# In the experts ScalarE makes a block's gate activation before the high part of the same slot

## The chip, the cores and the metric

One core of a Trainium2 chip runs the whole program. The metric is the device time of one execution in microseconds (us). The engines are named TensorE (PE in the profile, PEld for its weight loads), VectorE (DVE), ScalarE (ACT), GpSimd (POOL) and SyncE (SP), which issues most DMAs.

## What is computed

A trunk of two layers over 256 tokens of width 2048, all in float32. Each layer has an attention mixer and then a feed-forward part. In layer 0 that part is one dense SwiGLU; in layer 1 it is a mixture of 8 experts, of which every token takes its best two:

```python
def swiglu(x, wg, wu, wd):
    return (jax.nn.silu(x @ wg) * (x @ wu)) @ wd

def moe(xn, w_router, wg, wu, wd):
    ...
    for e in range(N_EXPERTS):
        y = y + comb[:, e:e + 1].astype(t.dtype) * swiglu(t, wg[e], wu[e], wd[e])
```

An expert has gate and up matrices of 2048 x 1408 and a down matrix of 1408 x 2048. The change touches the experts alone.

## The kernel before

**Pieces.** All weights come as pieces of 128 x 1024 float32 (512 KB), 920 of them, of which the last 528 are the experts' (8 times 66). SyncE loads each into one of 11 buffers of a ring (`load`, L394 to L400), as soon as TensorE has used the piece that was there 11 pieces before (semaphore `used`). ScalarE copies the piece to a rounded "high part" (`high`, L1032 to L1035: it waits for the landing, then one activation, tile `w_high`). VectorE makes the "low part", the piece less its high part (`low`, L1374 to L1378, tile `w_low`), which waits for the high part. TensorE then multiplies three times for each row block: high by high, high by low, low by high (`three`, L598 to L600), and counts the piece as used.

**Slots.** The order on each engine is written out by hand. An expert is a loop over 66 slots, 0 to 65; seven experts run in a hardware loop (`more` true), the last is written out once with 58 slots (`more` false). In slot i TensorE works on the expert's piece i + 8 (those from 66 on are the next expert's first eight), and ScalarE and VectorE prepare piece i + 14 (`ahead(e, i + 8, more)`, which adds `LEAD` = 6). So a piece prepared in slot i is multiplied in slot i + 6.

**Blocks.** The gate and up products come in 6 blocks: blocks 0 to 4 take 8 pieces each and give 256 columns of gate and 256 of up, block 5 takes 4 pieces and gives 128 and 128. Block 1 ends in TensorE's slot 7, block 2 in 15, 3 in 23, 4 in 31, 5 in 35, and the next expert's block 0 in slot 65 (`E_BLOCK_END = {7: 1, 15: 2, 23: 3, 31: 4, 35: 5, 65: 6}`). The down products follow in slots 36 to 57, eleven row blocks for each of 4 column blocks, two row blocks to a piece.

**From a block to the down products.** Five steps on three engines, each at a place fixed by its slot:

1. ScalarE, in the slot in which the block ends: `silu` (L1307 to L1310) waits on `used` for the block's last piece, then makes the gate activation (tile `silu_gate`).
2. VectorE, first thing in the next slot: `gated` (L1742) multiplies it with the up half (tile `h_blocks`).
3. TensorE, after the products of slot 3, 11, 19, 27, 34 or 37 for blocks 0 to 5 (`E_TURN`): transposes of `h_blocks` (L974), which wait for step 2.
4. ScalarE, one slot after the transposes and behind that slot's high part: the transposed block's high part (L1340, tile `hT_high`).
5. VectorE, two slots after the transposes and behind that slot's low part: its low part (L1771, tile `hT_low`). TensorE waits for this one before the down piece that first needs the block: for block 5 that is piece 5 of the down matrix, in slot 41.

So for block 5: block end and activation in slot 35, `gated` in 36, transposes after 37, `hT_high` in 38, `hT_low` in 39, needed in 41.

Each engine works its instructions in the order of the program, and an instruction that waits for a semaphore holds all behind it. The second pass over the experts (L1360 to L1362) runs only if one expert gets more than 128 tokens; here it does not run.

Of the kernel before, what the change touches and what calls it, by code (L numbers as in the profile page):

```python
# [101 lines left out]
def gu_width(b):  # L102
    return GW if b < 5 else P


def gu_chunks(b):
    return (2 * b, min(2 * b + 2, FC))


def gu_end(b):  # L110

    return 8 * (b + 1) if b < 5 else GU_PIECES
# [7 lines left out]
def dn_end(d):  # L120

    return GU_PIECES + (FC * (d + 1) - 1) // 2 + 1
# [29 lines left out]
def expert_groups(more, n_pass):  # L152


    tp, high = {}, {}
    for i in range(SLICE_PIECES):
        for kind, at in (("t", E_TURN), ("gather", E_GATHER if more else {}), ("st", expert_selt(more, n_pass))):
            if i in at:
                tp[kind, at[i]] = len(tp)
                if kind != "st":  # L160
                    high[kind, at[i]] = len(high)
    return tp, high


def trunk(nc, x, x_t, positions, gains, w_in, q_norm_dil, k_norm_dil, w_out, norm_ffn, ffn_dense, w_router, ffn_moe,
# [38 lines left out]
    with ExitStack() as ctx:  # L204
# [819 lines left out]
        def _(act):  # L1024
# [7 lines left out]
            def high(piece, shift=0):  # L1032

                act.wait_ge(raw_full[piece % RING], shift * (16 * SLICE_PIECES // RING) + 16 * (piece // RING + 1))
                act.activation(WH[:, piece % RING, :], RAWS[:, piece % RING, :], ACT.Copy).then_inc(high_done, 1)  # L1035
# [263 lines left out]
            def moe_pass(n_pass):  # L1299
                s = PASS[n_pass]  # L1300

                def ahead(e, i, more):

                    if more or i + LEAD < SLICE_PIECES:
                        high(s["piece"] + i + LEAD, e)

                def silu(e, b):  # L1307
                    act.wait_ge(used, e * SLICE_PIECES + (s["piece"] + gu_end(b % GU_BLOCKS) + SLICE_PIECES * (b // GU_BLOCKS)))
                    w = gu_width(b % GU_BLOCKS)
                    act.activation(SG[:, b % 2, 0:w], G[b % 2][:, 0:w], ACT.Silu).then_inc(silu_done, 1)  # L1310

                def gathered_high(count, k, q):
                    act.wait_ge(tp_ready, count + 1)
                    act.activation(XTH[:, 4 * q:4 * q + 4, 0:SLOTS], TP[k % 2][:, :].rearrange("p (c n) -> p c n", c=4),
                                   ACT.Copy).then_inc(tp_high, 1)

                def expert(e, more):
                    tp, _ = expert_groups(more, n_pass)
                    TP_MORE = s["tp_more"]
                    for i in range(SLICE_PIECES if more else NEXT_GU):  # L1320
                        ahead(e, i + 8, more)
                        if i in E_BLOCK_END:
                            silu(e, E_BLOCK_END[i])
                        if i in E_DOWN_END:
                            d = E_DOWN_END[i]
                            act.wait_ge(used, e * SLICE_PIECES + (s["piece"] + dn_end(d)))
                            if n_pass == 0:

                                if d == 0:
                                    act.wait_ge(cur_done, e + 1)  # L1330
                                act.activation(Y[:, d * NB:(d + 1) * NB], DN[d % 2][:, :], ACT.Copy,  # L1331
                                               scale=GC[:, 0:1]).then_inc(dn_free, 1)
                            else:
                                act.activation(YH[d % 2], DN[d % 2][:, :].rearrange("p (c n) -> p c n", n=P), ACT.Copy).then_inc(y_high, 1)
                        if i - 1 in E_TURN:
                            b = E_TURN[i - 1]
                            n = s["tp"] + tp["t", b]
                            c0, c1 = gu_chunks(b)
                            act.wait_ge(tp_ready, e * TP_MORE + (n + 1))
                            act.activation(HTH[:, c0:c1, 0:SLOTS], TP[n % 2][:, 0:(c1 - c0) * P].rearrange("p (c n) -> p c n", n=P),  # L1340
                                           ACT.Copy).then_inc(tp_high, 1)
                        if i - 1 in E_GATHER and more:
                            q = E_GATHER[i - 1]
                            n = s["tp"] + tp["gather", q]
                            gathered_high(e * TP_MORE + n, n, q)

                if n_pass:
                    for i in range(LEAD):
                        high(s["piece"] + i)
                for q in range(KD // 4):  # L1350
                    gathered_high(s["tp0"] + q, s["tp0"] + q, q)
                for j in range(8):
                    ahead(0, j, True)
                silu(0, 0)
                with act.Fori(0, N_EXP - 1) as e:
                    expert(e, True)
                expert(N_EXP - 1, False)

            moe_pass(0)
# [519 lines left out]
```

## Time and profile before

| | |
|---|---|
| median of three runs | 1936.08 us (1935.62 to 1936.53) |
| the profiled execution's own time | 1933.81 us |
| its span in the profile | 1931.7 us |
| TensorE (PE) busy | 1911.5 us, 99% |
| VectorE (DVE) busy | 1348.4 us, 70% |
| ScalarE (ACT) busy | 1163.4 us, 60% |
| chain that ended last | PE 92%, DVE 3%, DMA 2%, ACT 2% |

The share of busy time is a mean over stages. The experts take the last 750 us of the span, from about 1185 us on. Experts are numbered 0 to 7 here, and expert 3 starts its slot 0 near 1468 us. In a row of the timeline the time in square brackets is how long the engine sat idle before the instruction, and what ended that; a row without brackets followed the one before without idle time. Rows that merge several instructions say x2 or x3.

### The profile page before, as it was taken

Reading aid. Unit: us, or ns where it says so; the run is one execution under the profiler, and the core shown is the slowest. Engines: PE = TensorE matmul, PEld = TensorE weight load, DVE = VectorE, ACT = ScalarE, POOL = GpSimd, SP = SyncE. Lnnn points to the kernel's source line nnn. Section 1 sums busy time; section 2 is a strip of 40 time slices with the busy share of each in tenths; the row PEclk is TensorE's granted clock in tenths of the full one; section 3 lists DMA queues with packets and bytes.
Section 4 is the critical chain, followed back from the end, with each engine's and each line's share of the span. In section 5 each row is a group of like instructions: output and inputs, shape, how many; then the busy total and the mean of one; then the engine's idle time right before and its main releaser. Section 6 shows DMA issues by size and latency. Waiting matters only on the chain.

```text
span 1931.7 us, 27170 instructions
## 1 busy us (share of the span) xinstructions
PE 1911.5 (99%) x9176; PEld 1597.2 (83%) x9176; DVE 1348.4 (70%) x1580; ACT 1163.4 (60%) x1496; POOL 135.6 (7%) x152
## 2 busy tenths in 40 slices
PE   9999999999999999999999999999999999999998
PEld 7788888888888888888887888888888888888887
DVE  7776654554444555454657777898989898898996
ACT  7556543443433443444545557878878778787885
POOL 7300000000000000000200000000001000000101
PEclk9999999999999999999999999999999999999999
DMA  9555666666666666666665567999999999999997
GB/s 354 175 163 149 178 190 188 189 193 189 186 195 187 190 186 193 195 186 185 188 186 154 155 225 284 388 389 383 395 380 397 387 393 388 394 385 395 375 397 260
DMA packets 141588, 510.31 MB, mean 264 GB/s; under 512 B 15936, under 2 KB 15952, under 8 KB 140080
## 3 DMA queue, kind: packets, MB, share of 16 engines
q1 hardware_dynamic: 134288, 486.64, 72.3%
q0 software_dynamic: 7200, 22.39, 4.6%
q8 instruction: 56, 0.92, 0.2%
q14 instruction: 44, 0.36, 0.1%
HBM read 495.33 MB, written 13.64 MB: 263 GB/s over the span
## 4 chain that ended last, share of the span: by engine, by line
PE 92%; DVE 3%; DMA 2%; ACT 2%; issue 1%; SPq 0%; POOLq 0%; DVEq 0%; ACTq 0%
PE main L598 29%; PE main L600 29%; PE main L599 29%; DVE w_low L1377 1%; DMA raw_pieces<-in_w_in 1%; DMA raw_pieces<-in_ffn_moe 1%; PE transpose L934 1%; ACT w_high L1035 1%; PE transpose L616 1%; PE transpose L797 0%; PE transpose L974 0%; DVE heads_scratch L1417 0%; PE transpose L917 0%; DVE small L1418 0%; PE transpose L638 0%
## 5 line engine op out<-in xcount | busy, mean ns | idle before, releaser
L1377 DVE TENSOR_TENSOR w_low<-raw_pieces,w_high 128x1024 fp32r<-128x1024 f32 x919 | 1095.1, 1222 | 427.6 <-ACT w_high L1035 420.9
L1035 ACT ACTIVATE w_high<-raw_pieces 128x1024 fp32r<-128x1024 f32 x919 | 949.8, 1058 | 262.3 <-DMA raw_pieces<-in_ffn_dense 126.6
L598 PE MATMUL main<-w_high,xT_high 128*128 128x512 f32 (+1 forms) x1920 | 731.5, 381 | 2.5 <-DVE w_low L1498 0.9
L600 PE MATMUL main<-w_high,xT_low 128*128 128x512 f32 (+1 forms) x1920 | 721.5, 376 | 0.0
L599 PE MATMUL main<-w_low,xT_high 128*128 128x512 f32 (+1 forms) x1920 | 720.7, 375 | 0.0
L598 PEld LDWEIGHTS main<-w_high,xT_high 128*128 128x128 f32 x1920 | 361.8, 188 | 66.5 <-issue 3.3
L600 PEld LDWEIGHTS main<-w_high,xT_low 128*128 128x128 f32 x1920 | 361.6, 188 | 66.3
L599 PEld LDWEIGHTS main<-w_low,xT_high 128*128 128x128 f32 x1920 | 362.1, 189 | 62.8
L598 PE MATMUL main<-w_high,hT_high 128*128 128x512 f32 x832 | 329.9, 396 | 1.3 <-DVE hT_low L1771 1.2
L600 PE MATMUL main<-w_high,hT_low 128*128 128x512 f32 x832 | 324.6, 390 | 0.0
L599 PE MATMUL main<-w_low,hT_high 128*128 128x512 f32 x832 | 324.2, 390 | 0.0
L598 PEld LDWEIGHTS main<-w_high,hT_high 128*128 128x128 f32 x832 | 156.3, 188 | 35.0 <-DVE w_low L1377 3.9
L600 PEld LDWEIGHTS main<-w_high,hT_low 128*128 128x128 f32 x832 | 156.1, 188 | 33.3
L599 PEld LDWEIGHTS main<-w_low,hT_high 128*128 128x128 f32 x832 | 156.5, 188 | 30.4
L1259 ACT ACTIVATE silu_gate<-main,small 128x256 f32<-128x256 f32 (+1 forms) x48 | 19.3, 453 | 197.3 <-PE main L600 197.3
L588 POOL DMA_INDIRECT out_x<-attention_weights,result_rows x32 | 51.7, 1614 | 470.2 <-ACT attention_weights L1331 426.6
L1564 DVE TENSOR_TENSOR x_resid<-main,x_resid 128x512 f32<-128x512 f32 x32 | 20.6, 686 | 68.4 <-PE main L600 68.4
L554 POOL DMA_DIRECT2D heads_scratch<-in_q_norm_dil x1 | 0.6, 556 | 881.0 <-PE main L600 881.0
L1265 ACT ACTIVATE hT_high<-transpose 128x512 fp32r<-128x512 f32 (+1 forms) x24 | 13.5, 563 | 69.2 <-PE transpose L797 69.2
L1331 ACT ACTIVATE attention_weights<-main,slot_gates 128x512 f32<-128x512 f32 x32 | 22.0, 686 | 29.7 <-PE main L600 29.5
L1052 ACT ACTIVATE squares<-x_resid 128x512 f32<-128x512 f32 x32 | 20.2, 633 | 23.9 <-DVE x_resid L1564 18.2
L1063 ACT ACTIVATE xT_high<-transpose,gains_by_row 128x256 fp32r<-128x256 f32 x48 | 18.8, 475 | 21.7 <-PE transpose L616 21.7
(231 smaller groups left out, 812.7 us busy)
## 6 DMA issues: line engine op xcount, KB each, us to landing
raw_pieces<-in_ffn_moe SPq DMA_DIRECT2D x528, 512.0 KB, 6.4
raw_pieces<-in_ffn_dense SPq DMA_DIRECT2D x264, 512.0 KB, 3.7
raw_pieces<-in_w_in SPq DMA_DIRECT2D x96, 512.0 KB, 3.7
raw_pieces<-in_w_out SPq DMA_DIRECT2D x32, 512.0 KB, 3.6
x_resid<-in_x SPq DMA_DIRECT2D x4, 512.0 KB, 15.0
out_x<-x_resid POOLq DMA_DIRECT2D x4, 512.0 KB, 3.7
xn_rows<-token_major POOLq DMA_DIRECT2D x2, 1024.0 KB, 5.5
token_major<-in_x_t SPq DMA_DIRECT2D x1, 1024.0 KB, 10.0
```

The source lines that it names most:

```text
L588: pool.indirect_dma_start(out[d][:, :], bass.IndirectOffsetOnAxis(ap=RC[:, 0:1], axis=0), Y[:, cols], None, compute_op=ALU.add).then_inc(y ...
L598: pe.matmul(out_ap, lh[ls], rh[rs], start=first, stop=False)
L599: pe.matmul(out_ap, lh[ls], rl[rs], start=False, stop=False)
L600: return pe.matmul(out_ap, ll[ls], rh[rs], start=False, stop=last)
L616: ins = pe.transpose(TP[n % 2][:, (TILES * c + t) * P:(TILES * c + t + 1) * P], X[:, t, (2 * g + c) * P:(2 * g + c + 1) * P], IDN[:, :])
L934: ins = pe.transpose(TP[k % 2][:, i * P:(i + 1) * P], XG[:, c * P:(c + 1) * P], IDN[:, :])
L1035: act.activation(WH[:, piece % RING, :], RAWS[:, piece % RING, :], ACT.Copy).then_inc(high_done, 1)
L1052: act.activation(JUNK[:, :], X[:, t, d * NB:(d + 1) * NB], ACT.Square, accum_out=SSP[:, DBLOCKS * t + d:DBLOCKS * t + d + 1]).then_inc(sq_ ...
L1259: act.activation(SG[:, TILES * (b % 2) + t, 0:gu_width(b)], PAIR[b % 2][t][:, 0:gu_width(b)], ACT.Silu, scale=RSTD[1][:, t:t + 1]).then_in ...
L1331: act.activation(Y[:, d * NB:(d + 1) * NB], DN[d % 2][:, :], ACT.Copy, scale=GC[:, 0:1]).then_inc(dn_free, 1)
L1377: dve.tensor_tensor(WL[:, piece % RING, :], RAWS[:, piece % RING, :], WH[:, piece % RING, :], ALU.subtract).then_inc(low_done, 1)
L1564: dve.tensor_tensor(xs, PAIR[d % 2][t][:, :], xs, ALU.add).then_inc(dn_free, 1)
```

## The change

In ScalarE's slot loop of an expert, the call that makes the block's gate activation moves ahead of the call that makes the slot's high part. Nothing is added or removed. It touches the slots of `E_BLOCK_END`: six in each of seven experts, five in the last, 47 activations in all (the 48th, of the first expert's block 0, stands ahead of the loop).

```diff
                     for i in range(SLICE_PIECES if more else NEXT_GU):
-                        ahead(e, i + 8, more)
+
                         if i in E_BLOCK_END:
                             silu(e, E_BLOCK_END[i])
+                        ahead(e, i + 8, more)
                         if i in E_DOWN_END:
                             d = E_DOWN_END[i]
```

## Rows read from the trace of the kernel before

**Rows 1.** The page: TensorE's busy time, and the granted clock in 40 slices.
```profile
PE 1911.5 (99%) x9176; PEld 1597.2 (83%) x9176; DVE 1348.4 (70%) x1580; ACT 1163.4 (60%) x1496; POOL 135.6 (7%) x152
PEclk9999999999999999999999999999999999999999
```
**Rows 2.** Waits from 1200 to 1900 us: total us, times, longest.
```profile
ACT w_high L1035 <- DMA raw_pieces<-in_ffn_moe: 106.8, 302, 3.6
DVE w_low L1377 <- ACT w_high L1035: 67.3, 66, 3.4
...
ACT silu_gate L1310 <- PE main L600: 4.1, 8, 0.8
PEld main L598 <- DVE w_low L1377: 3.9, 7, 0.9
```
**Rows 3.** Waits from 1900 to 1903 us, in the last expert.
```profile
PEld main L598 <- DVE hT_low L1771: 0.2, 1, 0.2
```
**Rows 4.** Timeline of ScalarE, expert 3, slot 35: start us, us, instruction.
```profile
1517.04 1.06 ACT L1035 ACTIVATE w_high<-raw_pieces 128x1024 fp32r<-128x1024 f32 x1 [0.22 <-DMA raw_pieces<-in_ffn_moe]
1518.01 0.26 ACT L1310 ACTIVATE silu_gate<-main 128x128 f32<-128x128 f32 x1
```
**Rows 5.** Timeline of VectorE, expert 3, slots 33 to 39.
```profile
1515.67 3.69 DVE L1377 TENSOR_TENSOR w_low<-raw_pieces,w_high 128x1024 fp32r<-128x1024 f32 x3
1519.28 0.28 DVE L1742 TENSOR_TENSOR h_blocks<-main,silu_gate 128x128 f32<-128x128 f32 x1
1519.52 1.23 DVE L1377 TENSOR_TENSOR w_low<-raw_pieces,w_high 128x1024 fp32r<-128x1024 f32 x1
1520.66 0.42 DVE L1771 TENSOR_TENSOR hT_low<-transpose,hT_high 128x256 fp32r<-128x256 f32 x1
1520.99 3.49 DVE L1377 TENSOR_TENSOR w_low<-raw_pieces,w_high 128x1024 fp32r<-128x1024 f32 x3
1524.41 0.28 DVE L1771 TENSOR_TENSOR hT_low<-transpose,hT_high 128x128 fp32r<-128x128 f32 x1
```
**Rows 6.** Timeline of TensorE's matmuls, expert 3: the last of block 5.
```profile
1517.46 0.28 PE L600 MATMUL main<-w_high,xT_low 128*128 128x256 f32 x1
```
**Rows 7.** Timeline of TensorE's weight loads, expert 3, slots 40 and 41.
```profile
1524.10 0.19 PEld L600 LDWEIGHTS main<-w_high,hT_low 128*128 128x128 f32 x1
1524.81 0.19 PEld L598 LDWEIGHTS main<-w_high,hT_high 128*128 128x128 f32 x1 [0.53 <-DVE w_low L1377]
```
**Rows 8.** Timeline of ScalarE, expert 4, slot 35.
```profile
1612.08 0.28 ACT L1310 ACTIVATE silu_gate<-main 128x128 f32<-128x128 f32 x1 [0.23 <-PE main L600]
1612.25 0.38 ACT L1340 ACTIVATE hT_high<-transpose 128x256 fp32r<-128x256 f32 x1
```
**Rows 9.** Timeline of TensorE's matmuls, expert 4: the last of block 5.
```profile
1611.76 0.28 PE L600 MATMUL main<-w_high,xT_low 128*128 128x256 f32 x1
```
**Rows 10.** Timeline of ScalarE, expert 4, slots 15 and 16.
```profile
1582.03 1.06 ACT L1035 ACTIVATE w_high<-raw_pieces 128x1024 fp32r<-128x1024 f32 x1 [0.22 <-DMA raw_pieces<-in_ffn_moe]
1583.85 0.39 ACT L1310 ACTIVATE silu_gate<-main 128x256 f32<-128x256 f32 x1 [0.76 <-PE main L600]
1584.13 1.06 ACT L1035 ACTIVATE w_high<-raw_pieces 128x1024 fp32r<-128x1024 f32 x1
```
**Rows 11.** Timeline of VectorE, expert 4: the low part of slot 15.
```profile
1583.80 1.22 DVE L1377 TENSOR_TENSOR w_low<-raw_pieces,w_high 128x1024 fp32r<-128x1024 f32 x1
```
**Rows 12.** Timeline of TensorE's weight loads, expert 4: block 2's transposes, then slot 21's first.
```profile
1588.86 0.37 PEld L974 LDWEIGHTS transpose<-identity,h_blocks 128*128 128x128 f32 x2
...
1590.47 0.19 PEld L598 LDWEIGHTS main<-w_high,xT_high 128*128 128x128 f32 x1
```
**Rows 13.** Timeline of TensorE's matmuls in the two mixers: two long idle times.
```profile
64.17 1.08 PE L638 MATMUL transpose<-identity,token_major 128*128 128x128 f32 x4 [2.81 <-DVE token_major L1427]
...
1057.08 0.70 PE L660 MATMUL spread<-heads_scratch,incl 128*128 128x256 f32 x2 [1.28 <-DVE heads_scratch L1459]
```
**Rows 14.** Busy time in stretches: us, engines, granted clock (PEclk), DMA.
```profile
63.50:67.00 3.50, 2.83 (x9) 2.47 (x10) 1.78 (x2) 1.65 (x3) 2.77 (x9) 0.51 0.25 103
1050.00:1060.00 10.00, 8.72 (x41) 7.01 (x40) 8.56 (x14) 5.41 (x9) 0.00 (x0) 1.00 0.55 162
```

## The prediction, made before the changed kernel ran

> **What bounds the kernel.** I read the page first: TensorE is busy 99% of the span at the full clock in nearly every slice [rows 1], so an edit on ScalarE costs or gives only what it does to TensorE's few idle moments. The second view is the list of waits over the experts [rows 2]. ScalarE waits 302 times for a landing (106.8 us) and VectorE 66 times for a high part (67.3 us), and neither matters by itself, because both prepare a piece six slots before it is used. TensorE itself waits only in one kind of row: seven times, 3.9 us in all, longest 0.9, ended by VectorE; the last expert has an eighth of 0.2 [rows 3]. So there is one stop per expert. The third view, the timeline around one of them, says where: in expert 3 the weight load at 1524.81 comes 0.53 us late [rows 7], just after VectorE has ended block 5's `hT_low` at 1524.41 + 0.28 = 1524.69 [rows 5]. The profile names VectorE's next instruction as the one that ended the wait, but 1524.81 is 0.12 after the end of `hT_low`, which slot 41 needs. The weights of slot 41 were ready since 1519.36 (end of the third low part of the row at 1515.67).
>
> **What leads to that stop.** I follow VectorE back from 1524.41 [rows 5]. Low parts of slots 37 to 39, block 4's `hT_low`, the low part of slot 36, `gated` of block 5 and, before these, the low part of slot 35 follow each other with no idle time. The low part of slot 35 had to wait for its high part, which ScalarE ran from 1517.04 to 1518.10 after it had waited 0.22 us for the landing [rows 4]. From the start of that high part (1517.04) to the end of block 5's `hT_low` (1524.69) it is 7.65 us, of which the high part is 1.06 and the rest is VectorE at full load. Whatever delays the high part of slot 35 delays TensorE in slot 41, one for one.
>
> **What the change does there.** Slot 35 is a block end, so in the new order the high part stands behind an activation that waits for TensorE to end slot 35.
> - When does TensorE end it? In expert 3 the last matmul of block 5 starts at 1517.46 [rows 6]. Expert 4 shows what follows: last matmul at 1611.76 [rows 9], and the activation, which did wait there, at 1612.08 [rows 8], 0.32 later. So in expert 3 it can start at 1517.78, and ScalarE, free since 0.22 before 1517.04, now stands still for about 1 us although its piece has landed.
> - When does the high part follow? Behind the small activation the next instruction starts 0.17 later in expert 4 [rows 8]; behind the wide one of slot 15 a high part starts 0.28 later (1583.85 to 1584.13) [rows 10]. No row has a high part straight behind the small one. I take 0.22, nearest to both, with 0.15 and 0.32 as ends (0.32 is four hundredths more than the wide one needs).
> - The high part then starts at 1518.00 in place of 1517.04, 0.96 late. VectorE's chain has no idle time to give back, so `hT_low` ends at 1518.00 + 7.65 = 1525.65 and the load of slot 41 starts 0.12 later, at 1525.77. The load before it ends at 1524.10 + 0.19 = 1524.29 [rows 7]. The idle time becomes 1.48 us where it was 0.53.
>
> **The same in all eight.** Until now the stop hung on when the piece of slot 35 happened to land, which differs between experts: 0.2 to 0.9 us. In the new order the chain starts at TensorE's own last matmul of block 5 and ends at TensorE's slot 41, and what lies between is fixed: 0.32 + 0.22 + 7.65 + 0.12 = 8.31 us of chain, against 1524.29 - 1517.46 = 6.83 us of TensorE's own work. So each expert stops for 1.48 us. Where the high part used to run far ahead of TensorE, as in expert 4, it is delayed by more than in expert 3, but the old stop was shorter, and the new order ends at the same 1.48. The sum: 8 x 1.48 = 11.8 us new, less 3.9 + 0.2 = 4.1 us old, is +7.7 us. With the ends 0.15 and 0.32 for the step behind the activation the stop is 1.41 or 1.58, and the sum 7.2 or 8.5.
>
> **The step that the sum rests on** is that the high part can't pass the waiting activation. Rows 10 show one such hold: ScalarE stood idle for 0.76 us ahead of the activation of slot 15, and only then came the next high part. The Trainium skill says it outright (TensorE: Matmul & The Clock Gate, section "Architectural detail: the array is 16× 32×32, not 1× 128×128"): ScalarE's and VectorE's queues are strictly first in, first out, while TensorE may pull weight loads ahead. If a ready activation could pass a waiting one, the sum would be nothing in place of 7.7; the trace agrees with the page.
>
> **The other block ends** cost nothing that reaches TensorE. In slots 7, 15, 23, 31 and 65 either TensorE has ended the block before ScalarE comes to it (only 8 of the activations waited at all, 4.1 us together [rows 2]); then the activation fills part of a wait for a landing and the high part comes 0.3 us late at most. Or ScalarE is early and now waits longer. The worst I found is slot 15 of expert 4: the activation starts at 1583.85 as before, since TensorE sets it, and the high part, which ran at 1582.03, comes behind it at 1584.13, 2.10 late [rows 10]. Its low part can start at 1584.13 + 1.06 + 0.03 = 1585.22 in place of 1583.80 [rows 11], and end at 1586.44. TensorE takes up slot 21 at 1590.47 [rows 12]. That is 4.0 us of cover left. `gated` of block 2 moves by the same 1.42 us, to about 1586.8, and its transposes come at 1588.86 [rows 12]. Both costs are set at nothing; were the cover gone, such a slot would cost up to 2.1 us. Earlier gate activations bring nothing in these blocks, since their transposes have the same kind of cover. Block 5's own transposes get `gated` 0.96 us later, about when they are due, but a stop there only comes ahead of the stop in slot 41 and is part of it. No DMA is moved; SyncE's loads hang on TensorE's `used` alone, so they shift with TensorE and land no later relative to it.
>
> **Rivals.**
> 1. *No change.* The delayed high part of slot 35 is swallowed, since weights are ready six slots ahead and VectorE catches up. For it speaks the slack of the weights themselves (5 us in expert 3). Against it: VectorE's row has no idle time from slot 35 to 39, and what is late is not the weight but `hT_low` behind it. Time 1936.1. Chance 0.08. It becomes true if VectorE's chain has more than 0.9 us of idle time in the experts that stop now.
> 2. *Faster.* The activation in the gap of a landing wait saves ScalarE some 0.3 us a block, and the chain to slot 41 shortens until the old stops are gone: 4.1 us less, 1932.0. It needs TensorE to end block 5 before ScalarE arrives, and in expert 3 the last matmul starts 0.4 us after the high part does. Chance 0.02.
> 3. *Other block ends reach TensorE too.* If the delayed high parts of slots 7 and 15 eat the cover in the half of the experts where ScalarE is early, 4 more stops of up to 2.1 us come on top: 1943.8 + 8.4 = 1952.2. It decides only once 4.0 us of cover are gone. Chance 0.03.
> 4. *The clock falls.* After an idle time of 2.81 us in the first mixer [rows 13] the granted clock was 0.51, that is the lower level of 1.2 GHz, for the next 3.5 us [rows 14]; after 1.28 us in the second mixer [rows 13] it stayed at 1.00 [rows 14]. A stop of 1.48 us lies near the second. At the lower level half of 3.5 us is lost; eight times that is 14 us, 1957.8. Chance 0.02.
>
> **How the numbers follow.** The forecast is 1936.08 + 7.7 = 1943.8 us (for the profiled execution 1933.8 + 7.7 = 1941.5), with chance 0.85. The range for 8 times in 10 takes the ends 7.2 and 8.5, and adds for what one expert's rows can't tell of the others (another idle moment in VectorE's chain worth 0.35 us in each expert on the low side, 7.2 - 2.8 = 4.4; one slot's worn-out cover of 2.1 us on the high side, 10.6): 1940.5 to 1946.7. It leaves out all four rivals. A measurement of this kernel can tell about 0.2%, 3.9 us, from no change. Slower by more than that: the forecast and rivals 3 and 4, 0.90. Within: rival 1, 0.08. Faster: rival 2, 0.02.
>
> **What would show it.** In the waits of the new profile TensorE should have eight stops, all alike, near 1.5 us, at slot 41 (or split between block 5's transposes and slot 41); ScalarE's waits of `silu_gate` for TensorE should rise from 8 to well over 20; the expert's length should grow by 0.6 to 1.3 us each, with all growth between slots 35 and 41. If the stops stay unequal at 0.2 to 0.9, the chain as I read it is wrong; if they are equal but of another size, the step behind the activation is.

## The result and the profile after

| | before | after |
|---|---|---|
| median, 8 runs each | 1935.72 us | 1941.18 us |
| range | 1931.77 to 1937.0 | 1937.45 to 1943.17 |
| the profiled execution's own time | 1933.81 us | 1943.07 us |
| its span | 1931.7 us | 1941.0 us |

The medians lie 5.5 us apart. The ratio of the runs is 1.0031, with a 95% interval of 1.0023 to 1.0040, which makes the cost of the change 6.0 us, between 4.5 and 7.7. The ratios of this document leave out two executions that took far longer than all others (4983.57 us of the kernel in which only VectorE's order changes, 3789.71 us of the kernel before). The forecast was +7.7, slower; the range of 1940.5 to 1946.7 holds the time.

The two profiled executions lie 9.3 us apart, more than the medians. Of that, 2.2 us had come up before the experts: the first transposes of expert 0 start at 1191.02 after and at 1188.85 before. 1.6 us of it come up around the stop in the first mixer that [rows 13] show. The stop itself ended only 0.3 us later (64.49 against 64.17); 1.3 us more were lost behind it, where the granted clock stayed low for longer after the change. The third number from the end of a row is the granted clock, first before, then after:

```profile
67.00:70.50 3.50, 3.50 (x17) 2.91 (x17) 1.23 (x1) 1.05 (x4) 3.22 (x5) 1.00 0.57 135
```
```profile
67.00:70.50 3.50, 3.50 (x10) 2.68 (x9) 1.23 (x1) 0.46 (x1) 3.17 (x5) 0.57 0.52 146
```

The other 0.6 us are a longer wait of TensorE near 584 us (1.18 against 0.63). The program is the same in both kernels up to there, and among the traces of the other kernels of this document the experts' first transposes start anywhere from 1186.93 to 1191.11. So in what follows the experts are compared by a length of their own, from the first transposes of expert 0 to the last weight-high matmul of the down products. Before it runs from 1188.85 to 1923.79, 734.94 us. After, from these two rows of TensorE's timeline, it is 741.96 us, so the experts cost 7.0 us more:

```profile
1191.02 0.38 PE L974 MATMUL transpose<-identity,h_blocks 128*128 128x128 f32 x2
...
1932.98 0.39 PE L598 MATMUL main<-w_high,hT_high 128*128 128x512 f32 x1
```

The waits of the kernel after, from 1184 us on (us in total, times, longest); [rows 2, 3] hold the lines of before, for a window that starts at 1200:

```profile
ACT w_high L1035 <- DMA raw_pieces<-in_ffn_moe: 100.3, 258, 3.5
DVE w_low L1378 <- ACT w_high L1035: 79.2, 83, 2.4
...
ACT silu_gate L1310 <- PE main L600: 26.0, 24, 2.1
PEld main L598 <- DVE w_low L1378: 7.0, 7, 1.1
...
PEld transpose L974 <- issue: 3.8, 7, 0.7
PEld main L598 <- DVE hT_low L1772: 1.0, 1, 1.0
PEld transpose L974 <- DVE h_blocks L1743: 0.5, 1, 0.5
```

ScalarE's gate activation waits for TensorE 24 times in place of 9 (26.0 us, not 4.5, when the trace of before is taken from 1184 us on too). TensorE's weight loads wait in two places in each expert now: eight times 1.0 us in slot 41 (7.0 + 1.0) and eight times about 0.54 us at block 5's transposes (3.8 + 0.5). Before there was one place, with 4.1 us.

Expert 3, slot 35, on ScalarE after the change, against [rows 4]:

```profile
1519.97 1.06 ACT L1035 ACTIVATE w_high<-raw_pieces 128x1024 fp32r<-128x1024 f32 x1 [0.21 <-DMA raw_pieces<-in_ffn_moe]
1522.41 0.28 ACT L1310 ACTIVATE silu_gate<-main 128x128 f32<-128x128 f32 x1 [1.39 <-PE main L600]
1522.59 1.05 ACT L1035 ACTIVATE w_high<-raw_pieces 128x1024 fp32r<-128x1024 f32 x1
```

The same stretch on VectorE, against [rows 5]:

```profile
1523.67 1.22 DVE L1378 TENSOR_TENSOR w_low<-raw_pieces,w_high 128x1024 fp32r<-128x1024 f32 x1 [0.90 <-ACT w_high L1035]
1524.82 0.28 DVE L1743 TENSOR_TENSOR h_blocks<-main,silu_gate 128x128 f32<-128x128 f32 x1
1525.02 1.21 DVE L1378 TENSOR_TENSOR w_low<-raw_pieces,w_high 128x1024 fp32r<-128x1024 f32 x1
1526.15 0.41 DVE L1772 TENSOR_TENSOR hT_low<-transpose,hT_high 128x256 fp32r<-128x256 f32 x1
1526.48 3.48 DVE L1378 TENSOR_TENSOR w_low<-raw_pieces,w_high 128x1024 fp32r<-128x1024 f32 x3
1529.89 0.28 DVE L1772 TENSOR_TENSOR hT_low<-transpose,hT_high 128x128 fp32r<-128x128 f32 x1
```

And TensorE: the last matmul of block 5 (as [rows 6]), then the weight loads with the two stops (as [rows 7]):

```profile
1522.09 0.28 PE L600 MATMUL main<-w_high,xT_low 128*128 128x256 f32 x1
```
```profile
1525.22 0.14 PEld L974 LDWEIGHTS transpose<-identity,h_blocks 128*128 128x128 f32 x1 [0.52 <-issue]
...
1529.11 0.19 PEld L600 LDWEIGHTS main<-w_high,hT_low 128*128 128x128 f32 x1
1530.29 0.19 PEld L598 LDWEIGHTS main<-w_high,hT_high 128*128 128x128 f32 x1 [0.99 <-DVE w_low L1378]
1530.40 0.19 PEld L599 LDWEIGHTS main<-w_low,hT_high 128*128 128x128 f32 x1
```

Read in order: block 5's last matmul at 1522.09, the activation 0.32 later, the high part of slot 35 another 0.18 later, VectorE idle 0.90 for it and then at work without idle time up to 1530.17, and TensorE's load at 1530.29. The gated product ends at 1525.10 and the transposes' load follows at 1525.22, the first stop.

### The profile page after: what moved, and what is told of

Read it like the earlier page. It is cut to its first block, busy times and chain, and to the rows that moved or that the text cites. A ratio compares the mean times of both kernels' runs of the same rounds, so it can differ in the third digit from the quotient of the medians.

```text
span 1941.0 us, 27170 instructions
## 1 busy us (share of the span) xinstructions
PE 1915.0 (99%) x9176; PEld 1598.3 (82%) x9176; DVE 1347.8 (69%) x1580; ACT 1156.7 (60%) x1496; POOL 136.8 (7%) x152
## 4 chain that ended last, share of the span: by engine, by line
PE 91%; DVE 3%; POOL 2%; ACT 2%; issue 2%; DMA 0%; POOLq 0%; DVEq 0%
PE main L598 29%; PE main L600 29%; PE main L599 28%; DVE w_low L1378 1%; PE transpose L934 1%; ACT w_high L1035 1%; PE transpose L616 1%; PE transpose L797 0%; PE transpose L974 0%; PE transpose L917 0%; PE transpose L638 0%; DVE heads_scratch L1418 0%; DVE small L1419 0%; DVE hT_low L1772 0%; PE spread L660 0%
## 5 line engine op out<-in xcount | busy, mean ns | idle before, releaser
L1310 ACT ACTIVATE silu_gate<-main 128x256 f32<-128x256 f32 (+1 forms) x48 | 17.2, 358 | 26.1 <-PE main L600 26.0
```

## The experiments

The theory under test: all of the loss comes from slot 35, where the high part stands behind an activation that waits for TensorE, and VectorE's full queue carries the delay to block 5's low part in slot 41. The first rival: the other block ends share in it. The second: standing still costs on ScalarE as such, wherever VectorE stands. The third: the old stops are no fixed amount.

### Slot 35 alone, and all the others alone

```diff
-                        ahead(e, i + 8, more)
-                        if i in E_BLOCK_END:
+                        if i in E_BLOCK_END and i == 35:
+                            silu(e, E_BLOCK_END[i])
+                        ahead(e, i + 8, more)
+                        if i in E_BLOCK_END and not (i == 35):
                             silu(e, E_BLOCK_END[i])
```

> Only slot 35 has the new order; the five other block ends keep the old one. Theory (all of the loss comes from the high part of slot 35 standing behind the activation of block 5): the experts grow by the same 7.0 us as with the whole change (in its trace 9.2 us up to the last piece, of which 2.2 us lie ahead of the experts), each expert stops TensorE by 1.2 us between slots 35 and 41, in two parts, block 5's transposes and slot 41. ScalarE waits for TensorE ahead of the activation in slot 35 in all eight experts. Rival (the other block ends share in the loss): less than 5 us.

Measured over 10 runs: ratio 1.0026 (1.0016 to 1.0035) against the kernel before, +5.0 us. In its trace the experts take 741.71 us, 6.8 more than before, and TensorE's waits are those of the whole change (the timed runs alone, with 3.1 to 6.8 us, leave room for less than the rival's 5; the trace does not):

```profile
ACT silu_gate L1310 <- PE main L600: 13.1, 16, 1.9
PEld main L598 <- DVE w_low L1379: 7.0, 7, 1.0
...
PEld transpose L974 <- issue: 3.7, 7, 0.5
...
PEld main L598 <- DVE hT_low L1773: 1.0, 1, 1.0
PEld transpose L974 <- DVE h_blocks L1744: 0.5, 1, 0.5
```

So slot 35 makes the whole loss. The complement has the condition `i != 35` in both places.

> The complement: new order in slots 7, 15, 23, 31 and 65, old order in slot 35. Theory: the experts' time is that of the kernel before within 0.3 us, with stops of 0.2 to 0.9 us in slot 41 as before, although ScalarE waits for TensorE longer at these block ends and high parts come up to 2 us late there. Rival (these delays reach TensorE or reach slot 35 through VectorE's backlog): 2 us or more slower. Rival (the earlier activations help): over 1 us faster.

Measured over 10 runs: ratio 0.9996 (0.9987 to 1.0006), no change. But its trace has 2.3 us more in the experts (737.27 us), as much as the first rival asks for, all in slot 41 and at block 5's transposes of single experts. The expectation of 0.3 us failed, so two things were open: whether the old stops are the same in every execution, and whether the other ends set VectorE back.

### The kernel before, twice more

> The kernel before again, for a second trace of it. Open: its stops in slot 41 hang on when the piece of slot 35 lands. In its first trace they add up to 3.1 us over the eight experts, while the timed runs put the whole change at +5.5 us where its trace shows +7.0 in the experts. Theory (landings fall differently from execution to execution, and the first trace had few stops): other sizes of the eight stops, by up to 1 us in single experts, in the mean a sum of 4 to 5 us. Rival (the stops are the same in every execution): 3.1 us again, each within 0.1 us.

> The kernel before a third time. Theory: again other sizes of the eight stops, between 2 and 6 us in sum. Rival: 3.1 us as in the first trace.

The experts took 734.47 and 736.78 us, against 734.94 in the first trace. The waits of weight loads, first in the one, then in the other:

```profile
PEld main L598 <- DVE w_low L1377: 3.3, 7, 0.9
...
PEld main L598 <- DVE hT_low L1771: 0.2, 1, 0.2
```
```profile
PEld main L598 <- DVE w_low L1377: 5.1, 7, 1.1
...
PEld transpose L974 <- issue: 0.8, 1, 0.8
...
PEld main L598 <- DVE hT_low L1771: 0.2, 1, 0.2
```

Expert 1, for one, stopped for 0.90 us in the first trace and in these two for:

```profile
1336.06 0.19 PEld L598 LDWEIGHTS main<-w_high,hT_high 128*128 128x128 f32 x1 [0.32 <-DVE w_low L1377]
```
```profile
1337.80 0.19 PEld L598 LDWEIGHTS main<-w_high,hT_high 128*128 128x128 f32 x1 [1.06 <-DVE w_low L1377]
```

So the old stops add up to 4.1, 3.5 and 6.1 us of waits in the three traces. The texts above and below give 3.1 us for the first trace, and 2.6 to 4.9 us for all three: that counts TensorE's lost time, about 0.12 us less for each stop than the idle time of its loads (why is said in the part on the prediction). The expected mean of 4 to 5 us was too high (it is 3.5, and the experts' lengths have a mean of 735.4), but the sizes do vary, and not the new ones: in the new order the experts took 741.96 and 741.71. Against the mean of three the change costs 6.6 us in the experts, nearer to the 5.5 to 6.0 of the timed runs.

The old stops have a floor, too, which the prediction did not see. Where slot 35's piece lands early, the stop is 0.31 to 0.32 us all the same (seven cases in the three traces; 0.24 to 0.25 in the last expert, in each of them). Expert 4 of the first trace is one, and shows what sets it. ScalarE, first row, makes the high part of slot 36 behind block 5's activation, which waits for TensorE [rows 8]; VectorE, second row, stands idle for it ahead of slot 36's low part:

```profile
1612.52 1.06 ACT L1035 ACTIVATE w_high<-raw_pieces 128x1024 fp32r<-128x1024 f32 x1
```
```profile
1613.61 1.23 DVE L1377 TENSOR_TENSOR w_low<-raw_pieces,w_high 128x1024 fp32r<-128x1024 f32 x1 [0.30 <-ACT w_high L1035]
```

That low part starts 1.85 us after block 5's last matmul (1611.76), and 1.85 or 1.86 us after it in all ten cases of the floor. So the kernel before already has the fault that the change makes bigger: a high part behind an activation that waits. Before it is slot 36's high part, after it is slot 35's too.

### Slot 31 alone

As above with the condition `i == 31`.

> Only slot 31 has the new order. In the run with all ends but slot 35 in the new order, VectorE took up the low part of slot 35 without idle time before it in four experts (2, 3, 6, 7), never sooner than 2.13 us after block 4's transposes, though its high part was there up to 0.8 us sooner. Theory (ScalarE's wait in slot 31 sets VectorE back, and the backlog lasts to slot 35): with slot 31 alone the low part of slot 35 again starts no sooner than 2.13 us after block 4's transposes in any expert, and those experts stop by 0.3 to 0.4 us. Rival (the backlog comes from the earlier ends, slots 15 and 23): single experts start it at 1.6 to 1.9 us as in the kernel before.

In experts 1, 2, 3, 5 and 6 the low part of slot 35 started without idle time before it, each time 2.13 us after block 4's transposes; in the other three its own high part came later than that. Expert 6, VectorE in slots 32 to 36, where four low parts follow each other:

```profile
1799.63 4.62 DVE L1379 TENSOR_TENSOR w_low<-raw_pieces,w_high 128x1024 fp32r<-128x1024 f32 x4
1804.17 0.28 DVE L1744 TENSOR_TENSOR h_blocks<-main,silu_gate 128x128 f32<-128x128 f32 x1
```

The theory held: ScalarE's wait in slot 31 sets VectorE back, and the backlog lasts for the four slots to 35. It makes a floor under the stops, of 0.38 to 0.43 us in those experts (the loads' idle time), hardly above the 0.31 that the old order has anyway, and in sum nothing that shows: 735.27 us, in a single execution. In the whole change it is hidden, since slot 35's own wait sets VectorE's start at 3.11 us after block 4's transposes. What is left of the 2.3 us above is landings that fell late in that execution (experts 0, 1 and 4 began slot 35's high part behind a landing at 2.16, 1.93 and 1.80 us after block 4's transposes); the traces of before reach 2.25.

### The suspected cause doubled

```diff
+                        if i == 34:
+                            silu(e, E_BLOCK_END[35])
                         ahead(e, i + 8, more)
-                        if i in E_BLOCK_END:
+                        if i in E_BLOCK_END and i != 35:
                             silu(e, E_BLOCK_END[i])
```

> The suspected cause doubled: block 5's activation goes ahead of the high part of slot 34, one slot earlier still, so two high parts stand behind its wait; all other ends as before. Theory (each weight part that stands behind the wait sets VectorE's chain back by one low part, 1.14 us): TensorE is late by 1.23 + 1.14 = 2.4 us in each expert, most of it at block 5's transposes (1.5 us), 19 us in all, 14 to 16 us above the kernel before, about 1950. Rival (ScalarE has 0.2 us a piece to make up the delay, so the second part costs little): 1.4 us per expert, 7 to 8 us above. Rival (stops this long bring the lower clock): over 25 us above, with a granted clock below 1 in the experts.

Measured over 4 runs: 1948.95 us against 1936.59 beside it, ratio 1.0061 (1.0041 to 1.0081); the expected 14 to 16 us lie at the upper end of that interval, and in the trace the experts take 750.79 us, 15.9 more than before. The stops are now mostly at the transposes:

```profile
PEld transpose L974 <- issue: 11.6, 7, 1.7
...
PEld main L598 <- DVE w_low L1379: 6.9, 7, 1.0
...
PEld transpose L974 <- DVE h_blocks L1744: 1.6, 1, 1.6
PEld main L598 <- DVE hT_low L1773: 1.0, 1, 1.0
```

The step from one to two delayed high parts is 750.79 - 741.96 = 8.8 us, 1.10 per expert: one low part of VectorE (1.14 between starts), and not the 0.2 that ScalarE's share would be. How long ScalarE stood still did not matter: it was 2.91 us in slot 34 of expert 3 and 1.44 us in expert 0, and both met the same two stops (1.66 and 0.99 us). What stands behind its wait did. The clock did not fall, with loads idle for 1.66 us at a time (TensorE, 1200 to 1300 us: 98.19 busy, granted clock 1.00):

```profile
1200.00:1300.00 100.00, 98.19 (x472) 81.55 (x471) 86.66 (x93) 77.64 (x89) 7.50 (x5) 1.00 1.01 382
```

### VectorE's order, with the old and with the new order on ScalarE

In VectorE's slot 39 block 5's low part goes ahead of that slot's weight low part; `turned_block_low` holds the old lines word for word.

```diff
                         if b < GU_BLOCKS:
                             gated(b)
+                        if i == 39:
+                            turned_block_low(i)
                         ahead(e, i + 8, more)
...
-                        if i - 2 in E_TURN:
+                        if i - 2 in E_TURN and i != 39:
+                            turned_block_low(i)
```

> The old order on ScalarE; on VectorE, in slot 39 alone, the low part of block 5 (what TensorE waits for in slot 41) goes ahead of that slot's weight low part. Theory (the stop is VectorE's chain of weight low parts ahead of block 5's low part): that part comes 1.14 us earlier, the old stops of 0.1 to 0.8 us vanish, the experts take 3.1 us less, some 1932.6 us where the kernel before has 1935.7. Rival (the stop waits for the arrival of data, in ScalarE or the DMA, and VectorE's order is not what decides): stops as before, no change.

Measured over 9 runs: 1932.10 us, ratio 0.9985 (0.9975 to 0.9994); experts 732.40 us, 2.5 less than in the first trace where 3.1 were expected. No stop in slot 41 is left, but three at block 5's transposes, 1.0 us in all, in experts where slot 35's piece landed late; VectorE's row in expert 3 shows two weight low parts ahead of block 5's in place of three:

```profile
1521.68 2.35 DVE L1377 TENSOR_TENSOR w_low<-raw_pieces,w_high 128x1024 fp32r<-128x1024 f32 x2
1523.95 0.28 DVE L1750 TENSOR_TENSOR hT_low<-transpose,hT_high 128x128 fp32r<-128x128 f32 x1
```

So VectorE's order decides whether there is a stop in slot 41 at all. The landing decides only how much longer than the floor it is, and that alone did not make one here.

> The whole change on ScalarE, and on VectorE the same move in slot 39. Theory (two stops one after the other, 0.36 us at block 5's transposes from the late gated product, 0.87 us at slot 41 from the late low part): the second vanishes, being shorter than the 1.14 us won, the first stays at 0.36 in each expert; the experts take 8 x 0.36 - 3.1 = -0.2 us against the kernel before, so no change within 0.5 us, and 7 us less than the whole change. Rival (the loss is ScalarE's standing still as such): the time stays near that of the whole change, 7 us above the kernel before.

Measured over 10 runs: 1933.48 us, ratio 0.9989 (0.9979 to 0.9998); experts 734.70 us, 0.2 less than in the first trace of before, as expected. The timed runs are 2.1 us below the kernel before (0.4 to 4.1), which is better than the expected "no change within 0.5 us". Some 0.5 us of that is the first trace's low stops (the mean of three is 735.4); the rest stays open. ScalarE waits longer than in any kernel so far, and TensorE stops only at the transposes:

```profile
ACT silu_gate L1310 <- PE main L600: 30.6, 26, 2.8
...
PEld transpose L974 <- issue: 3.7, 7, 0.5
PEld transpose L974 <- DVE h_blocks L1743: 0.5, 1, 0.5
```

7.3 us of the experts are gone (741.96 to 734.70) with ScalarE's order untouched.

### The gated product early, and both moves

```diff
+                        if i == 35:
+                            b = 5
-                        if b < GU_BLOCKS:
+                        if b < GU_BLOCKS and i != 36:
                             gated(b)
```

> The whole change on ScalarE, and VectorE makes the gated product of block 5 in slot 35, ahead of that slot's low part, in the time in which it otherwise stands idle for the late high part. Theory (first stop: transposes wait for the gated product behind the late low part; second stop: VectorE's chain from the late high part): the first stop vanishes, and since the chain lacks the gated product's 0.24 us now, slot 41 stops for 1.23 - 0.24 = 1.0 us in each expert, 8 us in all, against 2.6 to 4.9 us in the three traces of the kernel before: 3 to 5 us slower than it. Rival (the gated product itself is what slot 41 waits for in the end): both stops go, no loss left.

Measured over 10 runs: ratio 1.0026 (1.0014 to 1.0037), +5.0 us; experts 741.52 us. The first stop is gone, and the whole loss has moved to the second, 9.2 + 1.2 us in eight waits:

```profile
PEld main L598 <- DVE w_low L1378: 9.2, 7, 1.7
PE main L598 <- DVE hT_low L1774: 7.1, 8, 1.3
PEld main L598 <- DVE hT_low L1774: 1.2, 1, 1.2
```

That is 1.26 us of idle time in most experts, or 1.14 of lost time where I had expected 1.0: the gated product left VectorE's chain, but the low part of slot 36 now came up against its own high part, so only about 0.1 of the 0.24 was won. In expert 0 the stop is 1.7 us, behind a piece that landed late. The rival, that the gated product is what slot 41 waits for in the end, fell.

> The whole change on ScalarE with both moves on VectorE: block 5's gated product ahead of the low part of slot 35, block 5's low part ahead of that of slot 39. Theory: no stop is left in any expert, whatever the landings do, since 1.0 us is less than the 1.14 us won; the time is 2.6 to 4.9 us below the kernel before, about that of the old order with the low part of block 5 moved alone, 1932. Rival (ScalarE's waits cost something of their own): above it by 2 us or more.

Measured over 10 runs: 1931.75 us, ratio 0.9981 (0.9972 to 0.9991) against the kernel before; experts 732.66 us. Seven experts have no stop in slot 41, expert 0 has one of 0.4:

```profile
ACT silu_gate L1310 <- PE main L600: 31.5, 26, 2.6
...
PEld main L598 <- DVE w_low L1378: 0.4, 1, 0.4
```

So "no stop in any expert, whatever the landings do" failed in expert 0: the piece of slot 31 landed late (ScalarE waited 1.27 us for it, up to 1230.35), and VectorE had not made up for it when slot 35 came. ScalarE stands still for 31.5 us ahead of gate activations here, longer than in any other of these kernels, and yet the experts' length is the shortest but one. This version and the old order with the one move on VectorE both beat the kernel before and the kernel after; between the two the intervals overlap.

## Why the prediction was right, step by step

- **One stop per expert, in slot 41, ended by block 5's low part behind VectorE's queue: right.** Moving that low part ahead of one weight low part took the stops away with ScalarE unchanged.
- **Last matmul to activation, 0.32 us: right.** After: 1522.09 to 1522.41.
- **Activation to high part, taken as 0.22 between 0.15 and 0.32:** 0.18.
- **High part to the end of block 5's low part, 7.65 us:** 7.58 (1522.59 to 1530.17). The release, 0.12: 0.12.
- **The same stop in all eight experts: right** (1.48 to 1.53 us of idle time in seven, 1.70 in expert 0). The high part of slot 35 starts 2.03 us after block 4's transposes in seven experts and 2.14 in the eighth. Only there, in expert 0, was a late landing what ended its wait; the sum had no such case.
- **A split with the transposes** was named as possible; it came, 0.52 at the transposes and 0.99 in slot 41 in expert 3, together 1.51 against the predicted 1.48. Over the eight experts the waits sum to 12.3 us against 11.8. That 1.51 lies so near to 1.48 is in part luck. By the measured steps the chain is 0.32 + 0.18 + 7.58 + 0.12 = 8.20 us, 0.11 shorter than predicted, and would leave one stop of 1.37; the split adds about as much again, because TensorE makes up some 0.12 us between its two stops.
- **"Whatever delays the high part of slot 35 delays TensorE in slot 41, one for one": true of expert 3, not of all.** Where the piece landed early, slot 36's high part set the old stop, and VectorE's chain had idle time ahead of slot 36's low part (0.30 us in expert 4). It did no harm to the forecast, which compares the sum of the old stops, as measured, with a new chain that starts at TensorE.
- **The sum, +7.7, was too large in one term.** I took loads' idle time for lost time one for one, 12.3 less 4.1 would be 8.2, and the experts' length grew by 7.0. The restart gives some back: after the stop the loads stand at 1530.29 and 1530.40, 0.11 apart, where they are 0.23 apart in steady running. The new order has two restarts in each expert, the old mostly one: 8 x 0.12 = 1.0 us less, 7.2 in all.
- **The old stops, 4.1 us, were taken from one execution.** Three give 3.5, 4.1 and 6.1. That is another part of the way from 7.7 to the 5.5 to 6.0 of the timed runs; the new level is fixed, the old one is not. With 6.6 us in the experts against the mean of three traces, 0.6 to 1.1 us stay open, within the interval (4.5 to 7.7). The expected growth of 0.6 to 1.3 us for each expert came as 0.5 to 1.1, least where the old stops were longest (experts 1 and 6).
- **The other block ends cost nothing: right for the time** (ratio 0.9996 alone), though I had missed that slot 31's wait reaches slot 35 through VectorE. In slot 15 of expert 4 the activation waited 1.77 us, and TensorE met no stop.
- **Rivals.** No change: fell; it needed more than 0.9 us of idle time in VectorE's chain, and the most that the first trace has there is 0.30. Faster: fell; it needed TensorE to end block 5 first. Other ends reaching TensorE: fell as priced, apart from slot 31's floor. Lower clock: fell, also at stops of 1.66 us.

## What to carry to other kernels

On an in-order engine the place of a wait matters by what is queued behind it and who waits for that: here 31.5 us of standing still cost nothing once VectorE had its two short jobs first, and the 13.1 us of the kernel with slot 35 alone cost nearly 7 in the experts. Before an instruction that waits moves ahead of one that doesn't, follow the second one's result through the other engines' queues to the next thing the bottleneck engine waits for; slack of six slots in one use of a queue says nothing on a short job that stands behind it in the same queue. The cheapest cure stood on another engine: let the short job that the bottleneck waits for go ahead of the long one it doesn't.

## What the runs showed of the hardware that I had not expected

- After a stop TensorE's first two weight loads stand 0.11 us apart in place of 0.23, so a stop costs about 0.12 us less than its idle time in the row.
- All these kernels have the same program up to the experts, and yet TensorE's long wait in the first mixer, and the clock behind it, differ from execution to execution. With slot 35 alone the wait was 1.35 us and the granted clock stayed at 1.00. In the traces of before and after it was 2.81 and 3.83 us: from 63.5 to 67.0 the clock was 0.51 and 0.50, and from 67.0 to 70.5 it was 1.00 and 0.57.
- In one and the same program the landing that slot 35 waits for differs from execution to execution, by up to 1.5 us for a single expert: expert 1's high part started 1.49, 0.14 and 1.64 us after block 4's transposes in three traces of the kernel before.
